# Gathering a share of the expert activations before the last phase of a PEER layer, with bounds on the indices, on one NeuronCore

## What is computed

```python
s1, i1 = lax.top_k(s[:, :, 0], TOPK_HALF)          # first keys, 8 heads
s2, i2 = lax.top_k(s[:, :, 1], TOPK_HALF)          # second keys
cand = (s1[..., :, None] + s2[..., None, :]).reshape(t, PEER_HEADS, 256)
top_s, ci = lax.top_k(cand, TOPK)                   # 16 experts of 16384 per head
experts = e1 * N_KEYS + e2                          # e1, e2: first and second key of each
g = jax.nn.softmax(top_s, axis=-1)
act = gelu(einsum('td,thkd->thk', x_tok, peer_u[experts]))
out = einsum('thk,thkd->td', act * g, peer_v[experts])
x = layer_norm(ALPHA * x + out, ln2_g, ln2_b)
```

## Time and profile before

| | |
|---|---|
| three runs, median (lowest to highest) | 1785.86 us (1783.36 to 1786.16) |
| the profiled execution, its own time | 1782.16 us |
| its span, first to last instruction | 1780.1 us |
| PE, DVE, ACT, POOL busy, share of the span | 97%, 79%, 48%, 30% |
| granted TensorE clock, mean | 0.992 of 2.4 GHz |
| DMA, mean over the span | 283 GB/s |
| up phase, down phase (from the trace) | about 440 to 1183 us, 1183 to 1770 us (last matmul) |

### The profile page before, as it was taken

How to read it: one execution, slowest core, us unless ns; L and a number is a source line. 1 busy time by engine, 2 the same in 40 slices (tenths; PEclk the granted TensorE clock), 3 DMA queues, 4 the chain that set the end, 5 groups by cost and what they waited for, 6 DMA issues and landing times.

```text
span 1780.1 us, 31392 instructions
## 1 busy us (share of the span) xinstructions
PE 1719.6 (97%) x11882; PEld 1575.1 (88%) x11882; DVE 1408.6 (79%) x1998; ACT 854.3 (48%) x1084; POOL 528.3 (30%) x342
## 2 busy tenths in 40 slices
PE   7999999899999999999999999999979999999997
PEld 7999987799999999999999999997767667778876
DVE  7999997687966777777777776457878788999987
ACT  5544445444544444444444444355445445455544
POOL 0000000487880000000000000016877778744421
PEclk9999999999999999999999999999999999999999
DMA  7787777677777777767777777998999999999994
GB/s 267 266 279 254 254 255 249 257 249 237 252 246 249 244 237 238 243 234 244 236 237 244 242 233 241 360 322 288 344 360 358 344 366 361 374 410 398 395 327 143
DMA packets 171984, 504.52 MB, mean 283 GB/s; under 512 B 19200, under 2 KB 35712, under 8 KB 170368
## 3 DMA queue, kind: packets, MB, share of 16 engines
q1 hardware_dynamic: 132256, 427.08, 69.5%
q0 software_dynamic: 22528, 67.19, 10.0%
q10 hardware_dynamic: 17120, 9.35, 1.7%
HBM read 490.98 MB, written 79.69 MB: 321 GB/s over the span
## 4 chain that ended last, share of the span: by engine, by line
PE 72%; POOL 12%; issue 6%; DMA 5%; DVE 4%; ACT 1%; DVEq 0%; POOLq 0%; SPq 0%; ACTq 0%
PE psum L1395 19%; PE psum L1396 19%; PE psum L1397 19%; POOL sp_coef L577 8%; PE psum L1566 3%; POOL rows L571 3%; PE psum L1568 3%; PE psum L1567 3%; PE psum L1532 2%; DMA rows<-v_rows,sp_idx 2%; DVE w_lo L831 1%; PE psum L1439 1%; PE psum L1441 1%; PE psum L1440 1%; DMA row_late<-v_rows,sp_idx 1%
## 5 line engine op out<-in xcount | busy, mean ns | idle before, releaser
L616 ACT ACTIVATE w_hi<-raw 128x1024 fp32r<-128x1024 f32 x570 | 603.2, 1060 | 732.6 <-PE psum L1397 490.0
L1395 PE MATMUL psum<-xt_hi,w_hi 128*128 128x256 f32 x2944 | 827.6, 281 | 11.5 <-DVE xt_lo L845 9.6
L1396 PE MATMUL psum<-xt_lo,w_hi 128*128 128x256 f32 x2944 | 823.0, 280 | 0.0
L1397 PE MATMUL psum<-xt_hi,w_lo 128*128 128x256 f32 x2944 | 822.7, 279 | 0.0
L831 DVE TENSOR_TENSOR w_lo<-raw,w_hi 128x1024 fp32r<-128x1024 f32 x502 | 608.9, 1222 | 222.9 <-ACT w_hi L616 221.3
L1395 PEld LDWEIGHTS psum<-xt_hi,w_hi 128*128 128x128 f32 x2944 | 554.8, 188 | 12.6 <-issue 12.0
L1396 PEld LDWEIGHTS psum<-xt_lo,w_hi 128*128 128x128 f32 x2944 | 554.7, 188 | 0.0
L1397 PEld LDWEIGHTS psum<-xt_hi,w_lo 128*128 128x128 f32 x2944 | 554.6, 188 | 0.0
L571 POOL DMA_INDIRECT rows<-v_rows,sp_idx x103 | 147.5, 1432 | 740.0 <-PE psum L1397 653.5
L1566 PE MATMUL psum<-w_hi,c_hi 128*128 128x512 f32 x752 | 303.8, 404 | 33.4 <-DVE w_lo L831 24.9
L1568 PE MATMUL psum<-w_hi,c_lo 128*128 128x512 f32 x752 | 299.6, 398 | 0.0
(11 more groups left out here) (162 smaller groups left out, 1094.4 us busy)
## 6 DMA issues: line engine op xcount, KB each, us to landing
raw<-in_u_w_dram SPq DMA_DIRECT2D x256, 512.0 KB
raw<-in_v_w_dram SPq DMA_DIRECT2D x172, 512.0 KB
v_rows<-in_v_w_dram SPq DMA_DIRECT2D x128, 512.0 KB, 5.2
raw_late<-in_v_w_dram SPq DMA_DIRECT2D x84, 512.0 KB
raw<-in_w_in_dram SPq DMA_DIRECT2D x80, 512.0 KB
raw<-in_w_out_dram SPq DMA_DIRECT2D x32, 512.0 KB
raw<-in_w_q_dram SPq DMA_DIRECT2D x32, 512.0 KB
hid_spill<-hid ACTq DMA_DIRECT2D x7, 1024.0 KB, 15.4
```

Of the source, the lines that this page charges most:

```text
L616: nc.scalar.activation(parts_of(slot_u)[0][:, :], raw_of(slot_u), ACT.Copy).then_inc(hi_done, 1)
L1395: mm(dst, hi_w[:, sl], xt_hi[:, kk, :], start=st, stop=False)
L1396: mm(dst, hi_w[:, sl], xt_lo[:, kk, :], start=False, stop=False)
L1397: i = mm(dst, lo_w[:, sl], xt_hi[:, kk, :], start=False, stop=en)
```

## The change

1. **The blocks trade places.** Block 0 is now the gathered one, block 1 goes through PE in chunks 0 and 1 (`blocks_of`, `x2_place`, `sel[:, ..., 0]`, the order of the last norm). Block 0's tokens are gated by batch 16 of 32.
2. **The dumps come earlier.** A dump waits for 16 batches of gates instead of 32, and `DUMP_TILES` is [68, 69, 70, 71, 82, 98, 114, 122, 126] instead of [115, ..., 121, 123, 126]. The first five (tiles 0 to 79, `EARLY`) go to `early_spill`, the rest to `late_spill`; the layout in DRAM is now tile, first key, token.
3. **The activations are gathered twice.** In up, POOL issues 128 gathers from `early_spill`; `bounds_check` makes each skip the elements whose index lies beyond tile 79. In down it issues 128 gathers again, from `late_spill`, after DVE has shifted the indices (`late_indices`), so that those below tile 80 lie beyond the bounds. `sp_coef` is set to zero first and lies in memory of its own. A repeat gets an index beyond both bounds and stays zero, so `pick_coefs` and its multiplication go; the indices wait for `sp_once`.
4. **Later loads.** `res` is loaded before unit 160 of down instead of 64, `ln2g` and `ln2b` before unit 176 instead of 104.

```diff
+DUMPS_EARLY = 5
+EARLY = DUMP_ENDS[DUMPS_EARLY - 1]
+SKIPPED = 2 ** 22
-DUMP_TILES = [115, 116, 117, 118, 119, 120, 121, 123, 126]
+DUMP_TILES = [68, 69, 70, 71, 82, 98, 114, 122, 126]
...
-                if n == 16 * RAW:
+                if n == 40 * RAW:
                     sp.wait_ge(x1_out, 16)
...
-                if n == 26 * RAW:
+                if n == 44 * RAW:
...
+            def gather_early():
+                for k in range(PICKS):
+                    nc.gpsimd.indirect_dma_start(
+                        sp_coef[:, k:k + 1], None, early_dram, bass.IndirectOffsetOnAxis(sp_idx[:, 0, k:k + 1], 0),
+                        bounds_check=EARLY * N_KEYS * P - 1, oob_is_err=False).then_inc(early_in, 16)
...
-                        sp_coef[:, k:k + 1], None, hid_dram,
-                        bass.IndirectOffsetOnAxis(sp_idx[:, 0, k:k + 1], 0)).then_inc(act_in[k // PICKS_IN], 16)
+                        sp_coef[:, k:k + 1], None, late_dram, bass.IndirectOffsetOnAxis(sp_idx[:, 0, k:k + 1], 0),
+                        bounds_check=(N_KEYS - EARLY) * N_KEYS * P - 1, oob_is_err=False)\
+                        .then_inc(act_in[k // PICKS_IN], 16)
             pool.wait_ge(idx_done, 1)
+            nc.gpsimd.memset(sp_coef[:, :], 0.0).then_inc(coef_zero, 1)
+            pool.wait_ge(coef_zero, 1)
+            pool.wait_ge(early_out, 16 * DUMPS_EARLY)
+            gather_early()
+            pool.wait_ge(late_idx, 2)
...
-                act.wait_ge(g_folded, NB)
+                act.wait_ge(g_folded, NB // 2)
...
-            def pick_coefs(n):
...
+            def late_indices():
+                dve.wait_ge(early_in, 16 * PICKS)
+                nc.vector.tensor_single_scalar(sp_idx[:, 0, :], sp_idx[:, 0, :], float(SKIPPED - EARLY * N_KEYS * P),
+                                               ALU.add).then_inc(late_idx, 1)
+                dve.wait_ge(late_idx, 1)
+                nc.vector.tensor_single_scalar(sp_idx[:, 0, :], sp_idx[:, 0, :], SKIPPED - 1, ALU.bitwise_and)\
+                    .then_inc(late_idx, 1)
...
                 if u == U_DOWN:
                     gate_tile_of(N_KEYS - 1)
+                    late_indices()
```

More of the change, by code:

```diff
@@ L105, in blocks_of @@
 def blocks_of(j):
-    return [0] if j < JOINED else [0, 1]
+    return [1] if j < JOINED else [0, 1]
 X1_ORDER = [(0, 0), (0, 1), (0, 2), (1, 0), (1, 1), (0, 3), (1, 2), (1, 3)]
 X1_HALF = 5
-LN2_VECTOR = [(1, 0), (1, 1), (0, 0), (0, 1), (0, 2)]
-LN2_POOL = [(1, 2), (1, 3), (0, 3)]
+LN2_VECTOR = [(0, 0), (0, 1), (1, 0), (1, 1), (1, 2)]
+LN2_POOL = [(0, 2), (0, 3), (1, 3)]
 RAW_LATE = 2
@@ L262, in build @@
         sp_row = sb("sp_row", [P, 2, PICKS], f32, route)
+        sp_once = sb("sp_once", [P, PICKS], f32, route)
         route.close()
@@ L341, in x2_place @@
         def x2_place(b, d):
-            return picked[:, d * DCH:(d + 1) * DCH] if b and d < JOINED else v_bank(d, b)
+            return picked[:, d * DCH:(d + 1) * DCH] if b == 0 and d < JOINED else v_bank(d, b)
         USED0, GLU0, S0, TAPS0 = 1, 2, 2, 1
@@ L735, in dump @@
                 c0, c1 = DUMP_ENDS[n - 1] if n else 0, DUMP_ENDS[n]
-                act.wait_ge(g_folded, NB)
+                act.wait_ge(g_folded, NB // 2)
                 if c1 > GATE0:
                     act.wait_ge(hid_done, c1 - GATE0)
-                act.dma_start(hid_tiles[:, c0:c1, :], hid[:, c0:c1, P:T]).then_inc(hid_out, 16)
+                if n < DUMPS_EARLY:
+                    act.dma_start(early_tiles[:, c0:c1, :], hid[:, c0:c1, 0:P]).then_inc(early_out, 16)
+                else:
+                    act.dma_start(late_tiles[:, c0 - EARLY:c1 - EARLY, :], hid[:, c0:c1, 0:P]).then_inc(hid_out, 16)
             def gates_out(m):
@@ L797, in _ @@
             n_normed = 0
-            for turn, b in enumerate((1, 0)):
+            for turn, b in enumerate((0, 1)):
                 act.wait_ge(ln_var, TB + turn + 1)
@@ L1177, in after @@
                 dve.wait_ge(sp_chain, n_sp[0])
-            first = sel[:, 0, TB - 1].rearrange("p h k -> p (h k)")
-            second = sel[:, 1, TB - 1].rearrange("p h k -> p (h k)")
+            first = sel[:, 0, 0].rearrange("p h k -> p (h k)")
+            second = sel[:, 1, 0].rearrange("p h k -> p (h k)")
             dve.wait_ge(tok_done, 1)
             dve.wait_ge(rt, R[0])
-            then(ts(sp_row[:, 0], second, float(P), sp_tok[:, 0:1], ALU.mult, ALU.add))
+            then(ts(sp_row[:, 0], first, float(P), sp_tok[:, 0:1], ALU.mult, ALU.add))
             then(stt(sp_row[:, 1], first, float(N_KEYS), second, ALU.mult, ALU.add))
             after()
-            then(stt(sp_row[:, 0], first, float(N_KEYS * P), sp_row[:, 0], ALU.mult, ALU.add))
+            then(stt(sp_row[:, 0], second, float(N_KEYS * P), sp_row[:, 0], ALU.mult, ALU.add))
             then(nc.vector.tensor_copy(numbers, sp_row[:, 1]))
-            after()
-            nc.vector.tensor_copy(sp_idx[:, :, :], sp_row[:, :, :]).then_inc(idx_done, 1)
             then(nc.vector.memset(sp_once[:, 0:TOPK], 1.0))
@@ L1194, in _ @@
                 n = h * TOPK
-                if h > 1:
-                    after()
+                after()
                 then(tt(differ[:, :, 0:n], sp_row[:, 1, n:n + TOPK].unsqueeze(2).to_broadcast([P, TOPK, n]),
@@ L1200, in _ @@
                 i = nc.vector.tensor_reduce(sp_once[:, n:n + TOPK], differ[:, :, 0:n], AX.X, ALU.min)
[L1201 to L1204, removed]
+                then(i)
+            after()
+            then(ts(sp_once[:, :], sp_once[:, :], float(-SKIPPED // 2), float(SKIPPED // 2), ALU.mult, ALU.add))
+            after()
+            then(tt(sp_row[:, 0], sp_row[:, 0], sp_once[:, :], ALU.add))
+            after()
+            nc.vector.tensor_copy(sp_idx[:, :, :], sp_row[:, :, :]).then_inc(idx_done, 1)
             dve.wait_ge(sel_tr, 1)
@@ L1278, in coef_lo @@
                 tt(lo_c[:, :, :], hid[:, mine, :], hi_c[:, :, :].bitcast(f32), ALU.subtract).then_inc(clo_done, 1)
[L1280 to L1283 removed]
+            def late_indices():
[5 more added lines that the diff above has]
+                    .then_inc(late_idx, 1)
             def pick(k):
[L1287 to L1289 removed]
+                dve.wait_ge(act_in[k // PICKS_IN], 16 * PICKS_IN)
                 dve.wait_ge(rows_in[k % ROWS], 16 * (k // ROWS + 1))
@@ L1354, in rstd_out @@
                 dve.wait_ge(ln_chain, chain[0])
-                nc.vector.memset(stats[:, 1, 0, 0:1], 0.0).then_inc(ln2_rstd, 1)
+                nc.vector.memset(stats[:, 0, 0, 0:1], 0.0).then_inc(ln2_rstd, 1)
             d = NCH - 1
-            dve.wait_ge(v1_done, 1)
+            dve.wait_ge(v0_done, 1)
+            chunk_stats(0, d, add_down(0, d), x2_in)
+            moments(0)
+            dve.wait_ge(ln2_in, 32)
+            c00 = centre2(0, 0)
+            inverse(0, TB + 1)
+            rstd_out()
+            c01 = centre2(0, 1)
+            scale2(0, 0, c00 + 1)
+            scale2(0, 1, c01)
+            dve.wait_ge(used, USED0 + U_END)
             chunk_stats(1, d, add_down(1, d), x2_in)
             moments(1)
-            dve.wait_ge(ln2_in, 32)
             c10 = centre2(1, 0)
-            inverse(1, TB + 1)
+            inverse(1, TB + 2)
             rstd_out()
@@ L1366, in _ @@
             scale2(1, 0, c10 + 1)
+            c12 = centre2(1, 2)
             scale2(1, 1, c11)
[L1368 to L1378, removed]
+            scale2(1, 2, c12)
         @block.tensor
@@ L1595, in _ @@
                         down(u, u, j, h, c_sets[coef_slot(g)], blocks_of(j), False, g == GROUPS - 1).then_inc(used, 1)
-            for b in (1, 0):
+            for b in (0, 1):
                 for g in range(G_LAST, GROUPS):
```

38 lines of the change are left out of this document (22 added, 16 removed).

## The result

The change makes the kernel slower: 1799.87 us median of 10 runs (1793.94 to 1807.99) against 1786.01 us (1782.85 to 1792.81, 10 runs) of the kernel before, ratio 1.0079, 95% interval 1.0058 to 1.0100. The profiled execution has a span of 1794.2 us against 1780.1, 14.1 us more. Both profiled executions are about 3.8 us faster than their kernel's median, so the two traces can be set against each other.

The account below looks back on a forecast made before the run. It took POOL's issue of gathers to bound the slow stretch of down; -30 - 5 + 5 + 8 = -22 us on 1782.16 gave 1760, and 1764 us as median, chance 0.44, range 1748 to 1810.

Parts of the forecast that it names:

- Rival 1: Activation gathers of down: skipping saves POOL nothing, only the ends move; 1789 us, 1774 to 1798, chance 0.35.
- Rival 2: Activation gathers of down: the bounds' check makes each gather longer; 1811 us, 1793 to 1840, chance 0.21.
- What bounds the kernel: Slow stretch of down, 1250 to 1545 us: POOL's issue, 4.10 us per pick, costs about 30 us.
- I take the middle, 0.30 us: Activation gathers of down: each saves 0.30 us by skipping 63% of its elements, between bounds of 0 and 0.60.
- The whole -30 us: Activation gathers of down: a pick falls from 4.10 to 3.65 us, under the next bound's 3.76, gaining 30 us.
- d = 0.2 us: Assumed extra time per bounded gather in down, a fifth of 0.95 us; over 110 gathers +22 us.
- the ends' +3: Start of down and later loads together, -5 + 8 = +3 us, if the gathers gain nothing.
- Start of down, -5: Activation gathers start earlier as the last dump lands sooner and POOL's halts may go: 0 to -15 us, taken -5.
- Later loads, +8: Late in down, after unit 160: 4.2 MB now load where DMA is full, 0 to +10.5 us, taken +8.
- Small elements' cost for DMA, +5: Gained stretch of down: remaining small elements take DMA capacity needed for the faster pace, 0 to +9 us, taken +5.
- Early gathers, 0: Up: 128 gathers from about 939 us at 1.64 us apiece end near 1150, while POOL is idle, costing 0.
- The cover of 36 us: Up: time between the early gathers' expected end near 1150 us and DVE's need at 1186.3, 0.28 us per gather.

Follow-up runs that it names:

- e3: Kernel before with one activation gather for each row gather in down instead of 1.5: 1758.99 us, ratio 0.9842.
- e12: Same kernel as e3, run again on another chip: 1754.26 us, ratio 0.9821.
- e2: Kernel before with bounds that no index exceeds on its 128 activation gathers: 1790.23 us, ratio 1.0017.
- e1: Changed kernel with res and the norm's weights loaded at their old places again: 1789.68 us, ratio 1.0008.
- e4: Kernel before with only the later loads of the change: 1793.14 us, ratio 1.0040.
- e5: Changed kernel with the loads back and bounds of 0 on down's activation gathers, so practically every element is skipped: 1788.54 us, ratio 1.0034.
- e6: Changed kernel with the loads back and one activation gather for each row gather instead of 1.5: 1762.72 us, ratio 0.9877.

## Why the prediction was wrong, step by step

It said 1764 us with 0.53 for faster; measured are 1799.87. The mechanism that I named for the stretch stands, and the forecast within it fell. That the range of 1748 to 1810 us holds the measured time is no merit of the forecast: its upper end was made of rivals 1 and 2. (Rival 1's own lower end, 1774, is a slip: 1786 - 15 is 1771, before any spread.)

- **What bounds the kernel: right.** POOL's issue, worth 30 us: e3 gave 28.8 (31.6 in e12). The arithmetic behind it had 3.3 us per pick against a next bound of 3.76; e3 shows 3.48 for POOL's own part and 3.64 in all.
- **"I take the middle, 0.30 us": this step failed.** I had bounds of 0 and 0.60 us for what a skipping gather saves, no row for it, and took the middle between ends far apart. Measured is a cost of 0.05 us (0.994 against 0.942 us), the same for about three eighths, about five eighths, practically all and none skipped. The whole -30 us goes with it. The nearest rows were the 0.94 us of a gather of 4 KB rows and of one of 4-byte elements: they show that bytes have no price on POOL. Both name 128 indices, so they couldn't tell whether a skipped index would still be paid for; it is. The Trainium skill's account in "DMA: Bandwidth & Descriptors", section "Anatomy of one DMA — SWDGE (gpsimd) path", of a fixed part that scales with nothing and no large part for descriptors, spoke for rival 1; its size of some 2 us holds for a whole DMA, and the shortest time of a late one from issue to landing here is 2.8 us.
- **Rival 2 was what happened, at its small end.** The kind of cost was priced with d = 0.2 us; with the measured 0.05 us it gives 110 x 0.05 = 5.5 us, and with the ends' +3 some 1794. The 5.6 us that the profile shows beyond that are 3.6 at the start of down, 1.6 in the stretch of gathers, which grew by 7.1, and 0.4 behind it. e2 alone measures 2.5 to 3 us, 0.17%, with an interval from -0.05 to 0.38%.
- **Start of down, -5: mis-sized.** It came to 1.4 us. The last dump took 11.3 us to land (chain of waits, issued at 1188.3) instead of 15.17, but this execution was 1.8 us later at the gate of tile 127, of which 1 us was there already at 24 us, at ACT's first `sig` (25.07 against 24.09). The halts of POOL among its first gathers stayed: 5.39 and 4.89 us, against 5.60 and 3.93; skipped elements make as many packets, but whether that is the reason is not shown.
- **Later loads, +8: right in mechanism, and in size as far as is known.** e1 against the change, 0.7%, 12.6 us; e4, 0.4%, 7 us; 8.4 us in the profile from the last gather to the end.
- **Small elements' cost for DMA, +5: wrong.** e5 and e6 show no relief from skipping more; the 357 GB/s were due to POOL's pace, as e3's 394 GB/s with all elements shows. As the stretch was not gained, the term couldn't arise in the change itself.
- **Early gathers, 0: right, with hardly any cover left.** I had priced the idle time at 0.31 us per gather from the mixed stretch; among themselves gathers have 0.79. The cover of 36 us fell to 8.
- **Chances.** Of the three cases the likeliest, 0.44, was the one that no row bore out. With the loads where they were, the rest of the change gains nothing: 1.0008 in e1, and 1.0034 in e5, where still more is skipped. That is rival 1's mechanism but for the 0.05 us.

## What to carry to other kernels

Where an engine issues many small indirect DMAs, count instructions, and don't expect skipped elements to make them cheaper: a bound that skips most of a gather's elements made it 0.05 us longer, and gathering twice doubles the issue. (What a gather that names fewer indices costs, no run here shows; all name 128.) Before moving such work elsewhere, see whether it can be spread in time beside the work that waits for it; one changed rate (1 instead of 1.5 per row) gave the 29 us that the whole change was after. And a load that rides free in a stretch bound by something else can have a price once it is moved to one where DMA is full: here 7 to 13 us.

## What was not expected of the hardware

- Activation gathers that follow one another directly make POOL halt for 2.0 to 4.8 us after every seventh, 66 us in all over 128 of them; mixed with row gathers, from 1250 to 1545 us, none of them waits longer than 0.9 us in that way. The cause is open. At the start of down in the kernel before, the first such halt, 5.60 us, also comes after the seventh; the second, 3.93 us, comes after the eighth behind it.
- A gather with practically all of its 128 elements out of bounds takes the same time on POOL and counts the same 32 packets as one with none.
- A gather's mean time on POOL tells little about the gather. The shortest is 0.94 us everywhere without bounds, the mean 1.34 in the kernel before, 1.46 in e3 and 1.37 in e12, the same kernel as e3. The two gathers of the earlier trace rows that start while DVE runs an operation with two inputs in SBUF take 1.96 and 2.02 us.
